# One row pair of the first FFN moved from the plain to the seven-product form, and one sum moved ahead of a wait

## What is computed

```
def swiglu(x, w_gu, w_down):
    g, u = jnp.split(x @ w_gu, 2, axis=-1)      # w_gu: 1024 x 5632, each half 2816 wide
    return (jax.nn.silu(g) * u) @ w_down        # w_down: 2816 x 1024

x = x + 0.5 * swiglu(rmsnorm(x, norm_ffn1_g), ffn1_w_gu, ffn1_w_down)   # first FFN
x = x + hybrid_mixer(rmsnorm(x, norm_mix_g), ...)
x = x + 0.5 * swiglu(rmsnorm(x, norm_ffn2_g), ffn2_w_gu, ffn2_w_down)   # second FFN
return rmsnorm(x, final_norm_g)                 # then the second block
```

## Time and profile before

| | |
|---|---|
| median of 3 runs | 1755.51 us |
| the profiled execution's own time | 1756.75 us |
| its span, first to last instruction | 1754.9 us |
| TensorE busy | 1747.8 us, 100% of the span |
| VectorE busy | 1235.1 us, 70% |
| ScalarE busy | 846.9 us, 48% |
| 512-column matmuls of lines 2047 to 2049 | 3 x (913 + 494 + 64) |
| 256-column matmuls of lines 2133 to 2135 | 3 x (1232 + 192 + 144) |

### The profile page before, as it was taken

How to read it: one execution, slowest core, us unless ns; L and a number is a source line. 1 busy time by engine, 2 the same in 40 slices (tenths; PEclk the granted TensorE clock), 3 DMA queues, 4 the chain that set the end, 5 groups by cost and what they waited for, 6 DMA issues and landing times.

```text
span 1754.9 us, 26584 instructions
## 1 busy us (share of the span) xinstructions
PE 1747.8 (100%) x10407; PEld 1535.6 (88%) x10407; DVE 1235.1 (70%) x1949; ACT 846.9 (48%) x1436; POOL 38.8 (2%) x38
## 2 busy tenths in 40 slices
PE   9999999999999999999999999999999999999998
PEld 7889989878888899988888998988877888989897
DVE  7949849666776557965795894976688677748474
ACT  6425626454333335743453562654655543727274
POOL 0000000000000000000000000000232000000000
PEclk9999999999999999999999999999999999999999
DMA  5233423432123232333323233334521233333232
GB/s 184 83 108 97 129 88 103 116 104 84 51 82 106 87 108 97 109 110 97 97 88 114 94 111 97 109 109 131 140 61 61 84 96 96 97 96 119 90 117 72
DMA packets 68427, 176.61 MB, mean 101 GB/s; under 512 B 8112, under 2 KB 9392, under 8 KB 68304
## 3 DMA queue, kind: packets, MB, share of 16 engines
q1 hardware_dynamic: 66576, 171.60, 31.9%
q10 hardware_dynamic: 1280, 2.08, 0.3%
q0 software_dynamic: 448, 1.24, 0.3%
HBM read 170.70 MB, written 2.10 MB: 98 GB/s over the span
## 4 chain that ended last, share of the span: by engine, by line
PE 97%; DVE 1%; ACT 0%; issue 0%; DMA 0%; DVEq 0%; ACTq 0%; POOLq 0%
PE ps L2047 19%; PE ps L2049 19%; PE ps L2048 19%; PE ps L2133 10%; PE ps L2134 10%; PE ps L2135 10%; PE ps L2069 2%; PE ps L2071 2%; PE ps L2070 2%; PE ps L2282 0%; PE ps L2412 0%; PE ps L2437 0%; PE ps L2079 0%; PE ps L2423 0%; PE ps L2285 0%
## 5 line engine op out<-in xcount | busy, mean ns | idle before, releaser
L2047 PE MATMUL ps<-Ahi,wh 128*128 128x512 f32 x913 | 358.7, 393 | 0.0
L2049 PE MATMUL ps<-Ahi,wl 128*128 128x512 f32 x913 | 355.4, 389 | 0.0
L2048 PE MATMUL ps<-Alo,wh 128*128 128x512 f32 x913 | 355.4, 389 | 0.0
L2133 PE MATMUL ps<-BThi,wh 128*128 128x256 f32 x1232 | 341.0, 277 | 0.0
L2134 PE MATMUL ps<-BTlo,wh 128*128 128x256 f32 x1232 | 340.7, 277 | 0.0
L2135 PE MATMUL ps<-BThi,wl 128*128 128x256 f32 x1232 | 340.6, 276 | 0.0
L543 ACT ACTIVATE wh<-raw 128x1024 fp32r<-128x1024 f32 (+1 forms) x206 | 213.1, 1036 | 229.0 <-PE ps L2049 195.1
L1149 DVE TENSOR_TENSOR wl<-raw,wh 128x1024 fp32r<-128x1024 f32 (+1 forms) x206 | 250.1, 1215 | 64.9 <-ACT wh L543 62.9
L2133 PEld LDWEIGHTS ps<-BThi,wh 128*128 128x128 f32 x1232 | 231.8, 188 | 0.0
L2134 PEld LDWEIGHTS ps<-BTlo,wh 128*128 128x128 f32 x1232 | 231.3, 188 | 0.0
L2135 PEld LDWEIGHTS ps<-BThi,wl 128*128 128x128 f32 x1232 | 231.3, 188 | 0.0
(11 more groups left out here) (345 smaller groups left out, 2700.7 us busy)
## 6 DMA issues: line engine op xcount, KB each, us to landing
raw<-in_w_gu SPq DMA_DIRECT2D x128, 256.0 KB, 2.9
raw<-in_w_d SPq DMA_DIRECT2D x32, 512.0 KB, 3.6
raw<-in_w_dn SPq DMA_DIRECT2D x32, 512.0 KB, 3.9
raw<-in_w_up SPq DMA_DIRECT2D x48, 256.0 KB, 2.8
raw<-in_w_gu SPq DMA_DIRECT2D x22, 512.0 KB, 3.6
raw<-in_w_d SPq DMA_DIRECT2D x16, 384.0 KB, 3.2
raw<-in_w_v SPq DMA_DIRECT2D x8, 512.0 KB, 3.9
raw<-in_w_cc SPq DMA_DIRECT2D x8, 512.0 KB, 3.6
```

Of the source, the lines that this page charges most:

```text
L2047: pe.matmul(ps, wh[:, c], hi[:, k, :], start=(k == 0), stop=False)
L2048: pe.matmul(ps, wh[:, c], lo[:, k, :], start=False, stop=False)
L2049: last = pe.matmul(ps, wl[:, c], hi[:, k, :], start=False, stop=(k == nb - 1))
L2133: pe.matmul(ps, whi[:, w], bhi, start=(new and kp == 0), stop=False, skip_group_check=not new)
```

## The change

`JS` goes from (7, 5) to (6, 5): in the first FFN row 6, the last plain one, becomes a pair. With `JS` the four steps kp move one row earlier in the first FFN: `normed` and `sums_of_blocks` of kp = 0 from row 2 to row 1 and so on, the last `low_blocks` from row 6 to row 5. The weight operands of the first pair come one row earlier too. Group 0 of the first FFN now has two pairs in a row. The fourth sum's tile becomes `TA[6]` in the first FFN (it is `TA[7]` before), and the last plain row uses `TA[7]`. In both FFNs `total(u + 2, 3)` moves ahead of the last plain row's waits for its `Ahi`, and so ahead of its `Alo`.

```diff
-JS = (7, 5)
+JS = (6, 5)
...
                     if 0 <= kp < 4:
                         sums_of_blocks(2 * f, kp)
+                    if j == JS[f] - 1:
+                        total(u + 2, 3)
                     dve.wait_ge(s["ev"], EVN[u + 1])
                     a_lo(38 * f + a, j - a, TA[6 + j % 2])
-                    if j == JS[f] - 1:
-                        total(u + 2, 3)
```

## The result

| | before | after |
|---|---|---|
| median of 14 runs each | 1755.66 us (1755.26 to 1757.49) | 1759.58 us (1757.88 to 1761.65) |
| fastest run | 1755.26 us | 1757.88 us |
| ratio | | 1.0022, 95% interval 1.0015 to 1.0028 |
| profiled execution, own time | 1756.75 us | 1759.0 us |
| its span | 1754.9 us | 1757.2 us |

The median rose by 3.9 us (0.22%). The profiled execution rose by only 2.3 us. These two numbers lead to different questions. The first is answered by the trace to the tenth of a microsecond; the second, why the timed runs lie higher than the trace, needed experiments.

The account below looks back on a forecast made before the run. TensorE, busy for 1747.8 of 1754.9 us, was taken as the bound. -1.34 + 3.4 + 0.05 - 0.15 = +1.96 us on the median of 1755.51 gave 1757.5 us, with an 8-in-10 range of 1755.9 to 1759.7.

Parts of the forecast that it names:

- slower by over 0.2%: Whole kernel: median above 1759.0 us, from the clock rival and most of the longer stall; chance 0.10.
- The pair in place of the plain row: TensorE, first FFN: a plain row of 10.88 us becomes a pair of 9.54 us, 1.34 us less.
- The stall: First FFN's first pair: VectorE's backlog delays ScalarE's tap, so product 2 starts 3.4 us late; bounds 2.9 to 4.0.
- The weights for the earlier pair: First FFN, rows 3 and 4: low weight parts still come in time, with 1.8 us of cover; cost nothing.
- The second pair: First FFN, two pairs in a row: a late matmul here and there, 0.05 us, between 0 and 0.2.
- The sum moved ahead: Second FFN: total(3) fills a VectorE wait, so two late matmuls shrink; 0.15 us less, between 0 and 0.25.
- The clock rival: Gap at 75 us: granted clock falls from 2.4 to 1.2 GHz, 3.4 us more, giving 1760.9 us; chance 0.05.
- The prediction's own sign of being wrong: Trace of after: a granted clock below 1.00 at 75 to 85 us would count against the forecast.
- The longer stall: First FFN, products 4 and 6 and the second pair wait again: another 1.8 us, giving 1759.3 us; chance 0.07.

Follow-up runs that it names:

- e3: Kernel after, with ScalarE's pair_hi(4) and tap(0) of the first pair ahead of the last plain row's Ahi, both FFNs; 1759.71 us, ratio 1.0022.
- e9: The kernel of e6 (kernel after, VectorE's first-FFN rows packed), timed again on another chip; 1755.56 us, ratio 1.0001.
- e4: Kernel before with only the fourth sum moved ahead of the last plain row's Alo, JS staying (7, 5); 1755.61 us, ratio 0.9998.
- e6: Kernel after, with low parts and total(1) on VectorE in the first FFN moved between times_r and low_blocks; 1757.43 us, ratio 1.0009.
- e8: Kernel before, with four useless ScalarE copies ahead of the first FFN's first tap, making a shorter gap; 1756.72 us, ratio 1.0006.
- e5: Kernel after without the sum's move: six plain rows in the first FFN, fourth sum where it stood before; 1761.06 us, ratio 1.0030.
- e7: Kernel before, with eight useless ScalarE copies ahead of the first FFN's first tap, making a long gap; 1759.37 us, ratio 1.0019.
- e10: The kernel of e6 with six in place of five useless warm-up matmuls ahead of the first unit; 1755.85 us, ratio 1.0001.
- e11: The kernel of e2 (kernel after, gap filled with matmuls), timed again in another session; 1759.27 us, ratio 1.0019.
- e1: The kernel after, unchanged, timed and profiled a second time; 1758.79 us, ratio 1.0021.
- e2: Kernel after, with 24 useless 256-column matmuls between products 1 and 2 of the first FFN's first pair; 1758.90 us, ratio 1.0020.

## Why the prediction was right, and where it was short

The time was forecast at 1757.5 us with a range of 1755.9 to 1759.7; the median was 1759.58, inside the range by 0.1 us. That it is inside is luck in part: it lies 2.1 us above the forecast and outside the forecast's own range (1756.6 to 1758.6), and with 0.22%, above 1759.0 us, it is the outcome "slower by over 0.2%", which was given 0.10. On the profiled execution the forecast was a span of 1756.9 and 1757.2 came. What was right is the mechanism of the stall; what was short is what comes on top of it.

**The pair in place of the plain row, -1.34 us.** Right. The first pair starts at 72.34; 72.44 was forecast. VectorE's row 1 began 0.11 us earlier too (33.05 against 33.16).

**The stall, +3.4 us.** Right in size, place and cause. The tap was forecast at 78.03 and came at 77.93; product 2 near 78.6 and came at 78.43; the stall is 3.45 us. The two parts of it, some 0.5 us in product 0 and the rest at product 2, came as 0.44 and 3.01. What made this term good was to take VectorE's pace from another place of the same program with the same order of work, the second FFN, rather than from a sum of durations: from row 1's start to the tap it forecast 46.00 - 1.13 = 44.87 us, and 77.93 - 33.05 = 44.88 came. e3 and e9 show that the backlog is the cause: with the tap moved ahead it is paid elsewhere, with the backlog taken away the stall falls to 0.6 us.

**The weights for the earlier pair, 0.** Right: TensorE has no wait between 60 and 72 us.

**The second pair, +0.05 us, and what else follows the gap.** This is the first step that fell short. No wait came, as forecast, but the two pairs run at 0.1178 us per matmul where the prediction took a pair's 9.54 us as fixed. The trace of the kernel before had the warning: the first three pairs of its second FFN, from 904.56 us on, take 9.86, 10.00 and 9.89 us, of which late matmuls explain 0.2, and the prediction read only the late matmuls. It is 0.6 us in the profile of after, and the down units start at 95.47 in place of 94.9 for just this reason. It also comes where nothing changed: in the second FFN's first three pairs for about 1.0 us in the profiles of before, after, e4, e6, e8 and e9, for less in e3, e5, e7, e10 and e11, and not in e1 and e2; in before's profile once more from 1683 to 1700 us (0.7 us), where after has none; and in after's in the pair at 1530 us (0.3 us), where before has none. So part of it cancels between the two profiles and hid there.

**The sum moved ahead, -0.15 us.** Right in kind. The late matmuls at 912.94 and 917.28 are gone. By the three pairs in the traces it is 0.13 us, by e4's fastest runs (1754.88 against 1755.19 us) about 0.3. A new late matmul of 0.08 + 0.08 us, at 1021.28, isn't the sum's: e5 has it and e4 doesn't, so it comes with the split.

**The sum of the trace.** -1.34 + 3.45 + 0.60 - 0.13 + 0.17 + 0.28 (the pair at 1530 us, 9.80 us against the usual 9.52) - 0.1 (the earlier start) - 0.67 (before's two pairs from 1681 us) is +2.3, and the spans differ by 2.3. Nothing is left over: what lies outside the pairs, from the first pair's start to the end, adds up to 1250.5 to 1250.8 us in all 13 profiles.

**The clock rival, given 0.05.** This is the step that failed. The argument against it was that the earlier trace rows show a granted clock of 1.00 in a stretch of 0.90 us without a new matmul and in the last 5 us of the program. The first of these is three times shorter than the gap that was forecast; e8 and e3, with gaps of 1.1 and 1.5 us, indeed have no run at 0.998, so it said nothing of 2.9 us. The second says only that the clock of this one execution held that long: TensorE's last matmul ends at 1750.25 us there and the clock falls at 1755.55, behind the span, 5.3 us later; at the same place of e4 it falls 2.6 us after the last matmul (1749.38 and 1751.98), of the other profiles after 3.2 to 5.2. Two rows of one execution can't exclude what comes in some; by the runs made since, the chance was near a third. The rival's price, 3.4 us if it happens, was about right for one execution (2.9 us for 6.8 us at 1.2 GHz in e1, 1.7 for 3.4 us in e5). The prediction's own sign of being wrong, a granted clock below 1.00 at 75 to 85 us, is absent in after's trace and present in e1's and e5's. What the rival had wrong is that it is not a yes or no for the kernel. It happens in some executions, and it moves the median by a part. The Trainium skill, "TensorE: Matmul & The Clock Gate", Part 1, lists the lower clock as the state that follows idleness and says that the moment at which the clock rises to the higher level at a kernel's start varies from run to run. e1's trace, with 0.50 behind the gap, agrees with the first, and the first entries of 1.00 between 3.9 and 10.6 us in the 13 profiles agree with the second. That the fall varies too is what e1 and after show, with 0.50 and 1.00 behind the same gap. The prediction had cited the first and let two unfit rows outweigh it.

**The longer stall, given 0.07.** It didn't come: no product behind product 2 waits in the kernel after. The range's upper end, which took part of this rival in, held the result by another cause.

**What stays open.** Of the median's +3.9 us, the balance of the trace with the slower pace in the first FFN gives -1.34 + 3.45 + 0.6 + 0.04, about 2.75, and the fastest runs of the two kernels are 2.6 us apart. The other 1.2 us are what makes a typical run differ from the fastest one. The clock falls are part of them: the 14 of 23 runs below 1.000 lie 1.3 us above the nine at 1.000 on average, so they are worth some 0.8 us of a mean. But e2, e11 and e3 have no run at 0.998 and the same median.

The profiles show only three things by which executions of one kernel differ: a fall in the gap (1.7 or 2.9 us), a cold start (2.2 us) and the slower pace (1.9 us in all in after, none in e1). Without these the spans of after (1757.2) and e1 (1758.4) are both 1755.3 to 1755.4 us, some 1757.2 as timed, 0.7 us below the fastest of the 23 runs; the same count for before gives 1755.1 as timed, 0.1 below its fastest. By this count none of the 23 runs of the kernel after was without some of the three. Why they come more often there, and in which share, wasn't settled. It isn't the gap's idleness alone, since filling it gave nothing. It isn't shown to be the 16 pairs as such either: e9 and e10 have them and are level with before, but e6, the same kernel as e9, was 1.9 us above in another session.

## What to carry to other kernels

When work is moved earlier, count the room of the engine that prepares it, from its own first instruction to the deadline, and take its pace from a stretch of the same program with the same order, waits included: that gave 3.4 us where 3.45 came, on an engine only 70% busy over the whole. The kernels with a gap of 2 to 3 us on the bounding engine lost more than its length here, so add a chance of about a third for half clock behind it, and 4% on the few matmul groups that follow. Then look for a wait of the preparing engine that its own later work can fill: 0.57 us a row, filled in four rows, and a better order in the last one took 2.9 of the 3.45 us away.

## What the runs showed of the hardware

- **Whether the granted clock falls after an idle stretch is a matter of the execution.** The same program with the same gap of 2.9 us kept 1.00 once and fell to 0.50 once; the lower level lasted 6.8 us in e1 and 3.4 us in e5. In e1 it fell while TensorE was idle, in e5 0.6 us after it had begun again. With gaps of 1.1 and up to 1.5 us (e8, e3) no run had a mean clock of 0.998. Behind the last matmul of the program, where nothing can be lost any more, it fell after 2.6 us in e4 and after 5.3 us in before.
- **256-column matmuls have two paces at the same granted clock of 1.00**, 0.113 and 0.1178 us. The slower one began behind a stall or a start that was 0.01 to 0.08 us late, lasted for 22 to 226 matmuls (226 is 2.7 pairs), and in other executions of the same stretch it didn't come. Between 0.113 and 0.1178 lie 4% of a stretch in which nothing waits and every instruction looks alike. What switches it wasn't found.
- **The views of the granted clock don't show a cold start.** e6's and e11's first 512-column matmuls run 0.426 us apart up to about 10.6 and 10.2 us while the windows read 1.00; the distances between starts tell, and the trace's first clock entry, which stands at just these times. It costs about 2.2 us where it comes, and can make runs with a mean clock of 1.000 differ.
- **A mean clock of 0.999 needs no loss.** e4's profile has it from 2.1 us at the lower level behind its last matmul.
- **The restart behind a wait takes 0.2 us.** In every gap ended by a tap here (0.3 to 3.0 us between starts) the first matmul came 0.14 us after the end of ScalarE's tap, and the next 0.19 us later in place of 0.11, so 0.08 us come on top of the wait; in e1, where the clock had fallen, the next came 0.35 us later.
- **Filling an idle stretch with matmuls keeps the clock and saves nothing by itself.** None of 22 runs of the filled kernel fell to 0.998, and their medians were no lower.
